# The first weight block is issued by ScalarE beside x, and the second comes and is split in halves

## What is computed

```python
def rmsnorm(x, g):
    x32 = x.astype(jnp.float32)
    y = x32 * lax.rsqrt(jnp.mean(x32 * x32, axis=-1, keepdims=True) + RMS_EPS)
    return (y * g.astype(jnp.float32)).astype(x.dtype)

def swiglu(x, w_in, w_out):
    gate, up = jnp.split(x @ w_in, 2, axis=-1)
    return (jax.nn.silu(gate) * up) @ w_out

x = x + 0.5 * swiglu(rmsnorm(x, ffn1_norm_g[l]), ffn1_w_in[l], ffn1_w_out[l])   # comes first
# then a mixer (mLSTM and SGU), a second FFN, a final norm, and a second model of two layers
# (FFN, pool and SSD mixer, FFN; FFN, MLA mixer, FFN, final norm)
```

## Time and profile before

| | before |
|---|---|
| median of the runs | 1618.41 us |
| span of the profiled execution, which is also its own time here | 1619.2 us |
| PE busy | 1605.0 us (99%) |
| DVE busy | 1221.3 us (75%) |
| ACT busy | 807.2 us (50%) |
| POOL busy | 48.4 us (3%) |
| mean DMA rate over the span | 225 GB/s |
| granted clock of PE, mean | 0.997 |

### The profile page before, as it was taken

One profiled execution on the slowest core, in us unless ns is written; L12 is line 12 of the kernel. 1 busy time (PEld: TensorE's weight loads), 2 busy tenths in 40 slices (PEclk: granted clock), 3 DMA queues, 4 the chain that ended last, 5 costly groups with the idle time before them and its releaser, 6 DMA issues.

```text
span 1619.2 us, 33790 instructions
## 1 busy us (share of the span) xinstructions
PE 1605.0 (99%) x14157; PEld 1583.5 (98%) x14157; DVE 1221.3 (75%) x1382; ACT 807.2 (50%) x892; POOL 48.4 (3%) x81
## 2 busy tenths in 40 slices
PE   9999999999999999999999999999999999999998
PEld 9999999999999999999998999999999998899998
DVE  6888786676778878887777888877889578774544
ACT  5434567654644354443567654445444466654343
POOL 0000000000000000000000000000000010000000
PEclk9999999999999999999999999999999999999999
DMA  8788544444568865888453368874798535345551
GB/s 327 289 305 306 219 175 171 150 156 160 184 255 294 311 224 209 316 326 295 153 183 130 131 246 327 304 292 160 288 342 316 195 139 197 135 157 206 183 197 63
DMA packets 51066, 365.04 MB, mean 225 GB/s; under 512 B 5792, under 2 KB 5920, under 8 KB 7072
## 3 DMA queue, kind: packets, MB, share of 16 engines
q1 hardware_dynamic: 40176, 287.03, 48.5%
q0 software_dynamic: 10368, 75.50, 12.8%
q10 hardware_dynamic: 432, 1.20, 0.2%
HBM read 362.65 MB, written 1.05 MB: 225 GB/s over the span
## 4 chain that ended last, share of the span: by engine, by line
PE 95%; DVE 2%; ACT 1%; DMA 1%; issue 1%; DVEq 0%; SPq 0%; ACTq 0%
PE bank L261 54%; PE bank L297 27%; PE bank L253 3%; PE bank L280 2%; PE bank L2149 1%; PE bank L384 1%; DVE wlo L192 1%; PE bank L395 1%; DMA raw<-stream_in 0%; PE bank L1652 0%; PE bank L429 0%; PE bank L2195 0%; PE bank L2101 0%; PE bank L2119 0%; PE bank L1130 0%
## 5 line engine op out<-in xcount | busy, mean ns | idle before, releaser
L261 PE MATMUL bank<-xh,whi 128*128 128x256 f32 x2608 | 725.3, 278 | 1.3 <-DVE wlo L192 1.3
L261 PE MATMUL bank<-xl,whi 128*128 128x256 f32 x2608 | 721.6, 277 | 0.0
L261 PE MATMUL bank<-xh,wlo 128*128 128x256 f32 x2608 | 721.5, 277 | 0.0
L192 DVE TENSOR_TENSOR wlo<-raw,whi 128x2048 fp32r<-128x2048 f32 x254 | 580.9, 2288 | 180.5 <-ACT whi L184 180.2
L184 ACT ACTIVATE whi<-raw 128x2048 fp32r<-128x2048 f32 x253 | 482.8, 1913 | 277.3 <-PE bank L261 166.4
L261 PEld LDWEIGHTS bank<-xh,whi 128*128 128x128 f32 x2608 | 489.9, 188 | 2.6 <-DVE wlo L192 1.7
L261 PEld LDWEIGHTS bank<-xl,whi 128*128 128x128 f32 x2608 | 490.3, 188 | 0.1
L261 PEld LDWEIGHTS bank<-xh,wlo 128*128 128x128 f32 x2608 | 489.9, 188 | 0.0
L297 PE MATMUL bank<-hid_hi,whi 128*128 128x256 f32 x1056 | 292.1, 277 | 0.0
L297 PE MATMUL bank<-hid_lo,whi 128*128 128x256 f32 x1056 | 291.6, 276 | 0.0
L297 PE MATMUL bank<-hid_hi,wlo 128*128 128x256 f32 x1056 | 291.6, 276 | 0.0
(11 more groups left out here) (392 smaller groups left out, 1842.8 us busy)
## 6 DMA issues: line engine op xcount, KB each, us to landing
raw<-stream_in SPq DMA_DIRECT2D x269, 1024.0 KB, 4.9
mod_raw<-mod_in POOLq DMA_DIRECT2D x72, 1024.0 KB, 7.6
params<-params_in SPq DMA_DIRECT2D x1, 1474.0 KB, 9.5
x<-x_in SPq DMA_DIRECT2D x2, 512.0 KB, 4.7
raw<-stream_in SPq DMA_DIRECT2D x2, 512.0 KB, 6.6
m_gsu<-sgu_in ACTq DMA_DIRECT2D x1, 1024.0 KB, 4.7
y_out<-y_tiles SPq DMA_DIRECT2D x4, 256.0 KB, 2.9
consts<-consts_in SPq DMA_DIRECT2D x1, 280.5 KB, 7.2
```

Of the source, the lines that this page charges most:

```text
L192: dve.tensor_tensor(wlo[:, s, :], raw[:, s, :], whi[:, s, :].bitcast(F32), ALU.subtract)\
L261: last = pe.matmul(out[:, m, :], (whi, wlo)[wp][:, s, k * 256 + m * P:k * 256 + m * P + P], (xh, xl)[ap][:, k, :], start=(k == 0 and j == ...
```

## The change

ACT's program begins with the first half of block 0, then the gain, then the second half of block 0; SP issues only x at the start. SP then waits for the first half of block 0 (`w_loaded_part`) and no longer for x, and issues block 1 in halves, block 2, and consts behind it. ACT and DVE split block 1 in halves. PE runs block 0 in the order whi x xh and whi x xl for k 0 to 3, the same for k 4 to 7, then wlo x xh for all k; the 12 small products between are gone. The counting of later halves is raised by one.

```diff
@@ halves_index
-                n_halves += 1
+                n_halves += 2 if n == 0 else 1
@@ def pe_first_block(pe, out):
-            for part, (w, xs) in enumerate(((whi, xh), (whi, xl), (wlo, xh))):
+            for part, k0, k1 in ((0, 0, 4), (1, 0, 4), (0, 4, 8), (1, 4, 8), (2, 0, 8)):
+                w, xs = ((whi, xh), (whi, xl), (wlo, xh))[part]
                 if part == 2:
                     pe.wait_ge(sem("w_lo_ready"), 1)
-                for k in range(KD):
+                for k in range(k0, k1):
                     if part == 0 and k == 0:
                         pe.wait_ge(sem("w_half_ready"), 1)
                     if part == 0 and k == 4:
-                        pe_start_warm(pe, 12)
                         pe.wait_ge(sem("w_hi_ready"), 1)
@@ act_ffn_later, n == 0
                 act_squares(act, 0)
-                act_split(act, 1)
+                act.wait_ge(sem("w_loaded_part"), 32)
+                act.activation(whi[:, 1, 0:H], raw[:, 1, 0:H], ACT.Copy).then_inc(sem("w_half_ready"), 1)
+                act.wait_ge(sem("w_loaded1"), 16)
+                act.activation(whi[:, 1, H:BLK], raw[:, 1, H:BLK], ACT.Copy).then_inc(sem("w_hi_ready"), 1)
                 act.wait_ge(sem("x_loaded1"), 16)
                 act_squares(act, 1)
@@ dve_ffn_later, n == 0
                 dve_first_remainders(dve)
                 dve_split(dve, 0)
-                dve_split(dve, 1)
+                dve.wait_ge(sem("w_half_ready"), 2)
+                dve.tensor_tensor(wlo[:, 1, 0:H], raw[:, 1, 0:H], whi[:, 1, 0:H].bitcast(F32), ALU.subtract)
+                dve.wait_ge(sem("w_hi_ready"), 2)
+                dve.tensor_tensor(wlo[:, 1, H:BLK], raw[:, 1, H:BLK], whi[:, 1, H:BLK].bitcast(F32), ALU.subtract)\
+                   .then_inc(sem("w_lo_ready"), 1)
                 dve_fold_squares(dve, n)
@@ block.sync
             for i in range(2):
                 sp.dma_start(x[:, 4 * i:4 * i + 4, :], a_x[:, 4 * i:4 * i + 4, :]).then_inc(sem(f"x_loaded{i}"), 16)
-            sp.dma_start(raw[:, 0, 0:H], a_stream[0:P, 0:H]).then_inc(sem("w_loaded_part"), 16)
-            sp.dma_start(raw[:, 0, H:BLK], a_stream[0:P, H:BLK]).then_inc(sem("w_loaded0"), 16)
-            sp.wait_ge(sem("x_loaded1"), 16)
-            for n in range(1, SLOTS):
-                sp.dma_start(raw[:, n, :], a_stream[n * P:n * P + P, :]).then_inc(sem(f"w_loaded{n}"), 16)
-                if n == 1:
-                    sp.dma_start(consts[:, :], a_consts).then_inc(sem("consts_loaded"), 16)
+            sp.wait_ge(sem("w_loaded_part"), 16)
+            sp.dma_start(raw[:, 1, 0:H], a_stream[P:2 * P, 0:H]).then_inc(sem("w_loaded_part"), 16)
+            sp.dma_start(raw[:, 1, H:BLK], a_stream[P:2 * P, H:BLK]).then_inc(sem("w_loaded1"), 16)
+            sp.dma_start(raw[:, 2, :], a_stream[2 * P:3 * P, :]).then_inc(sem("w_loaded2"), 16)
+            sp.dma_start(consts[:, :], a_consts).then_inc(sem("consts_loaded"), 16)
@@ block.scalar
+            act.dma_start(raw[:, 0, 0:H], a_stream[0:P, 0:H]).then_inc(sem("w_loaded_part"), 16)
             act.dma_start(params[:, 0:4 * KD], a_params[:, 0:4 * KD]).then_inc(sem("gain_loaded"), 16)
+            act.dma_start(raw[:, 0, H:BLK], a_stream[0:P, H:BLK]).then_inc(sem("w_loaded0"), 16)
             act.wait_ge(sem("eps_ready"), 3)
```

## The result

The changed kernel takes 1622.08 us (median of 22 runs, 1618.94 to 1626.95); the kernel before, now with 22 runs, 1618.41 (1616.13 to 1623.63). The ratio is 1.0017, with a 95% interval of 1.0010 to 1.0025: slower by 1.6 to 4.1 us, which is a small loss and, by the bound of 0.5%, no change. Two later series of runs gave 1.0012 (0.9992 to 1.0031) and 1.0008 (0.9990 to 1.0027). The mean of the differences of means over the three series, each weighted by its scatter, is +2.8 us with a standard error of 0.45. The forecast was 1618.4 with a range up to 1621.6: the time lies above it.

A forecast was written before the change was run, and what follows sets the result against it. Only the moment PE begins its second block, 17.30 us, was taken to bound the end. With the gain landing at 7.65 it became 17.35, +0.05 on 1618.41, given as 1618.4; range 1615.4 to 1621.6.

The forecast's parts named there:

- What bounds: Whole run: only the moment PE begins its second block, 17.30 us, can move the end; PE is busy 99%.
- Part 1: Start: three edits shorten the chain through block 1's load; PE could start block 1 at 15.3, at most 2.1 us gained.
- (a): SP's start: issue block 1 when block 0's first half has landed, not x; wait expected to end about 6.5 again.
- Part 2: Start: the gain waits behind weights on ACT's queue, DVE has no slack; block 1 at G + 9.7, break-even G 7.6.
- How late is G: Gain's landing on ACT's queue: bounded between 5.4 and 8.0, narrowed to 7.3 to 8.0, middle 7.65 taken: +0.05 us.
- rival 2: Start: gain lands later than the same bytes today, about 9.2; block 1 at 18.9, +1.6 us, 1620.0; chance 0.13.
- Part 3: Other edits: removing the 12 small products brings nothing, extra DMA issues cost nothing, no later PE wait depends on absolute time.
- Rival 3: PE's clock falls because its work at the start gets too thin; loses 3 us, 1621.4; chance 0.06.

The follow-up runs named there:

- e6: Kernel before with two idle products on DVE ahead of wlo of block 1, about 1.5 us of delay: ratio 1.0022, +3.3 ± 1.0 us.
- e7: Kernel before with five idle products on DVE ahead of wlo of block 1, about 4.7 us of delay: ratio 1.0048, +8.4 ± 0.7 us.
- e14: Repeat of e12 (all weights on SP, no wait, block 1 in halves, new product order) against the kernel before: ratio 0.9987, -2.6 ± 0.6 us.
- e16: As e14, but with the old product order and the 12 small products in block 0; against the kernel before: ratio 0.9988, -2.9 ± 0.6 us.
- e2: Changed kernel with ACT issuing the gain ahead of the first half of block 0; against the kernel before: ratio 1.0016, +2.7 ± 1.1 us.
- e3: Changed kernel with all weights on SP and the wait for x kept; against the kernel before: ratio 1.0015, +1.8 ± 1.2 us.
- e13: Changed kernel with the gain issued by SP between the halves of x; against the kernel before: ratio 1.0003, -0.2 ± 0.6 us.
- e12: Kernel before with all weights on SP without the wait for x, block 1 in halves, new product order: ratio 0.9989, -2.1 ± 1.2 us.
- e8: Kernel before with only the new product order in block 0, without the 12 small products: ratio 1.0006, +1.5 ± 0.8 us.
- e4: Kernel before with only the new issue: block 0's halves from ACT, SP waiting for the first half; ratio 1.0026, +4.1 ± 1.1 us.
- e10: Changed kernel with 136 small warming products ahead of block 0 in place of 100; against the kernel before: ratio 1.0010, +1.0 ± 1.1 us.
- e11: As e2, but SP issues block 1 without waiting for the first half of block 0; against the kernel before: ratio 1.0007, +0.1 ± 1.2 us.
- e1: Changed kernel run again, unmodified, against the kernel before: ratio 1.0012, +2.2 ± 1.1 us.
- e9: Changed kernel run a third time, unmodified, against the kernel before: ratio 1.0008, +1.5 ± 1.0 us.
- e5: Kernel before, unchanged, run as the kernel under test: ratio 1.0004, +0.2 ± 0.6 us.
- e15: Kernel before, unchanged, run once more as the kernel under test: ratio 1.0003, 0.0 ± 0.9 us.

## Why the prediction was wrong

*What bounds* was right as far as the profiles go: the start of block 1 is carried on unchanged for the next 560 us, and e6, e7, e14 and e16 show it in the times. e2, e3 and e13 don't, so the times hold something else of 1 to 3 us as well. That block 1 starts at 17.30 was read from one profile as if it were a constant; it lies between 16.1 and 18.6, 16.9 in the mean. This is the first error, 0.4 us, and it hid in the base of the sum.

*Part 1* was right in size: without the late gain block 1 starts at 15.4 to 15.6 (15.3 was said), with all weights on SP's queue (e3, e12, e14). With the change's own two queues and the gain first it was 16.55 (e2), because (a) was wrong: the wait for the first half of block 0 ended at 7.7 and not at 6.5.

*Part 2*, the mechanism, was right term by term. With G = 9.20: wlo of block 0 at G + 4.92 (G + 4.94 said), PE's block 0 at G + 2.8 (2.9), block 1 at G + 9.53 (9.7). No idle time on DVE, no wait for block 1 by ACT.

*How late is G* is the step that failed; G is the moment at which the gain lands. The upper bound of 8.0 was the landing of the same bytes today, and the step allowed only for a gain on it, since the engines stood 0.35 idle between 2 and 4 us; the middle, 7.65, was taken. It is 9.20. The bound held bytes fixed and rate too, and the rate was the thing that the change touches: 186 and 270 GB/s from 2 to 6 us in place of 193 and 397, 0.27 MB less, which is 0.7 us at 397. The other 0.5 stays open. A bound "from the same bytes" is no upper bound when the bytes come in another way. The time for G = 9.2 stood in rival 2, at 18.9 and +1.6, for another reason (a further 512 KB ahead) and with a chance of 0.13.

The Trainium skill's rule ("DMA: Bandwidth & Descriptors", "Issuing engines are not separate DMA queues") was nearer than my middle: only issuing time is saved. By it G would have been 8.0, and even this was too kind: here a second queue did not merely save nothing, it slowed x (its halves landed at 7.5 and 9.0 in place of 5.2 and 6.5).

*Part 3*: the small products were free, as said, where PE waits for block 1 (e8), and cost at most 0.16 where it doesn't (e16). *Rival 3*, the clock, came up once (e4) and once by force (e7).

*The size of the loss*: the late G alone would have given rival 2's 1620.0, which is inside the range. The measured 1622.08 is 2.1 above that: 0.4 is the base, and the rest has no term in the prediction. Over the three series the start explains 1.8 ± 0.4 of the 2.8 ± 0.45 measured, and 1.0 is left, one and a half of its errors. A part is the higher heap: without all runs above 1624 us (a bound chosen afterwards) the three differences are 2.9, 1.6 and 1.5, in the weighted mean 2.2 ± 0.35, of which the start leaves 0.4. A lower clock in some executions, as in e4, could be a part too; e10 was too coarse to tell. It stays open.

## What to carry to other kernels

Look at what small load everything waits for, and keep it ahead of the large ones on its queue: here 16 KB placed behind 512 KB cost more than all that was won by splitting. In e12 and e14 the loads on one queue landed in the order of their issue, at 386 to 401 GB/s from 4 to 6 us; on two queues each delayed the other (e11, e13). So a first try is to keep the large loads on one queue in the order in which they are wanted, and to split the last one: e12, e14 and e16 do this and lie 2.1 to 2.9 us below the kernel before, a small gain (0.9987, 0.9975 to 0.9999 for e14) that under the bound of 0.5% is no change. And where the sum is of 1 to 2 us, take the base from several profiles: a landing of one execution is not the kernel's.

## What was not expected of the hardware

- Two loads of 512 KB issued at the same moment on SP's and ScalarE's queue: 262 to 283 GB/s from 4 to 6 us in six profiles, 386 to 409 in all others, also where ScalarE's large load came 0.45 us later behind a small one (399, 403).
- PE's products come in one of two spacings at the same granted clock: 267 or 257 in 30 us. In the fifth feed-forward layer the slower one held for the whole layer, about 6 us, in 5 of 18 profiles. What switches it was not found.
- The lower clock near 608 us, 6.8 us long in the first profile of before, lasted 3.4 in e1, e4, e6, e9 and others and was absent in e2, e5, e7, e8 and e15. With it PE was 3.4 us further behind e15 after that norm than ahead of it in the first profile of before, and 1.2 in e1, e4, e6, e10 and e13: a good part of an execution's scatter of some 2 us.
